# Every chunk of the SSM's GLU product as high and low halves

## What is computed

```
y = gelu(y.reshape(bsz, s, 512)).astype(u.dtype)      # 256 x 512
z_out, z_gate = split(y @ w_glu, 2, axis=-1)          # w_glu: 512 x 2048
y_ssm = z_out * sigmoid(z_gate)
```

## Time and profile before

| | |
|---|---|
| median of three runs | 1860.93 us |
| the profiled execution | 1868.62 us |
| its span | 1866.8 us |
| TensorE busy | 1796.2 us (96%) |
| VectorE busy | 1217.6 us (65%) |
| ScalarE busy | 871.8 us (47%) |
| GpSimd busy | 282.4 us (15%) |

### The profile page before, as it was taken

The page is one execution under the profiler, slowest core; times in us unless marked ns, Lnnn a source line. Parts: engine busy times, 40 slices in busy tenths (PEclk is TensorE's granted clock), DMA queues, the critical chain, the costliest instruction groups (busy, mean ns, idle before and its releaser), DMA issues.

```text
span 1866.8 us, 27009 instructions
## 1 busy us (share of the span) xinstructions
PE 1796.2 (96%) x10038; PEld 1444.8 (77%) x10038; DVE 1217.6 (65%) x1782; ACT 871.8 (47%) x1421; POOL 282.4 (15%) x278
## 2 busy tenths in 40 slices
PE   7999999989999999999989999999999999999998
PEld 6676667679998856667579998657899874779987
DVE  7997756555667893857556566545677744466775
ACT  4224445364444422436455445345655543565553
POOL 4115453010000003545111000110000001010000
PEclk9999999999999999999999999997999999799999
DMA  6445443445555444444245666431455544135553
GB/s 160 135 134 158 135 147 102 147 130 173 174 185 180 124 127 147 136 148 157 90 147 159 183 187 194 145 109 61 135 174 179 192 149 132 53 119 171 181 190 135
DMA packets 192358, 274.60 MB, mean 147 GB/s; under 512 B 25616, under 2 KB 129540, under 8 KB 192228
## 3 DMA queue, kind: packets, MB, share of 16 engines
q1 hardware_dynamic: 191364, 269.86, 46.8%
q0 software_dynamic: 864, 3.02, 0.5%
HBM read 271.78 MB, written 1.05 MB: 146 GB/s over the span
## 4 chain that ended last, share of the span: by engine, by line
PE 85%; DVE 8%; ACT 4%; issue 2%; POOL 1%; DMA 1%; DVEq 0%; ACTq 0%; SPq 0%; POOLq 0%
PE bank L402 51%; PE bank L400 23%; PE bank L590 2%; PE bank L676 2%; DVE WL L1181 2%; PE bank L1053 1%; PE bank L598 1%; PE bank L1033 1%; PE bank L492 1%; PE bank L876 1%; ACT WH L1476 1%; DVE HTL L2194 1%; DVE HTL L2111 1%; ACT HTH L1476 0%; PE bank L725 0%
## 5 line engine op out<-in xcount | busy, mean ns | idle before, releaser
L1181 DVE TENSOR_TENSOR WL<-W,WH 128x1024 fp32r<-128x1024 f32 x312 | 382.3, 1225 | 247.3 <-ACT WH L1476 238.9
L1476 ACT ACTIVATE WH<-W 128x1024 fp32r<-128x1024 f32 x332 | 351.8, 1060 | 272.8 <-PE bank L402 240.2
L402 PE MATMUL bank<-HTH,WH 128*128 128x256 f32 x1536 | 438.4, 285 | 11.6 <-issue 4.0
L402 PE MATMUL bank<-HTL,WH 128*128 128x256 f32 x1536 | 434.7, 283 | 0.0
L402 PE MATMUL bank<-HTH,WL 128*128 128x256 f32 x1536 | 434.7, 283 | 0.0
L402 PEld LDWEIGHTS bank<-HTH,WH 128*128 128x128 f32 x1536 | 294.6, 192 | 16.4 <-issue 10.0
L402 PEld LDWEIGHTS bank<-HTL,WH 128*128 128x128 f32 x1536 | 294.7, 192 | 0.2
L402 PEld LDWEIGHTS bank<-HTH,WL 128*128 128x128 f32 x1536 | 294.6, 192 | 0.0
L402 PE MATMUL bank<-WH,HTL 128*128 128x512 f32 x672 | 261.9, 407 | 0.0
L402 PE MATMUL bank<-WH,HTH 128*128 128x512 f32 x480 | 193.6, 403 | 6.9 <-DVE HTL L2194 5.0
L402 PE MATMUL bank<-WL,HTH 128*128 128x512 f32 x480 | 189.0, 394 | 0.0
(11 more groups left out here) (406 smaller groups left out, 2481.1 us busy)
## 6 DMA issues: line engine op xcount, KB each, us to landing
W<-in_w_in SPq DMA_DIRECT2D x132, 512.0 KB, 3.7
W<-in_ffn_w_gate_up SPq DMA_DIRECT2D x176, 256.0 KB, 3.4
W<-in_w_up SPq DMA_DIRECT2D x176, 256.0 KB, 3.4
W<-in_ffn_w_down SPq DMA_DIRECT2D x44, 512.0 KB, 4.2
W<-in_w_down SPq DMA_DIRECT2D x44, 512.0 KB, 4.2
W<-in_w_out SPq DMA_DIRECT2D x32, 512.0 KB, 3.3
W<-in_ssm_w_glu SPq DMA_DIRECT2D x16, 512.0 KB, 4.3
W<-in_x_w_kv SPq DMA_DIRECT2D x16, 512.0 KB, 3.8
```

Of the source, the lines that this page charges most:

```text
L402: m = pe.matmul(out, at_a(a[x]), at_b(b[y]), start=(start and i == 0), stop=(stop and i == 2), skip_group_check=True)
L1181: eng.tensor_tensor(WL[:, m % HSLOTS, 0:width], W[:, n % RSLOTS, 0:width], h, ALU.subtract)\
L1476: copy = lambda dst, src, scale=1.0: act.activation(dst, src, ACT.Copy, scale=scale)
```

## The change

All eight chunks of the GLU product go in halves. g0, g2, g4 and g6, whole before, become `"dve"` chunks: ScalarE makes their high half and VectorE the low one. GpSimd makes the halves of column tiles 0 and 1 of `UT` as well, under a new semaphore `glu_first`, for which TensorE waits ahead of `glu(0)`. In GpSimd's program this stands behind the splits of gate 3, with a wait for `y_ready` ahead of it, and the splits of gates 4 and 5 follow it.

```diff
+        glu_first = (OTR[:, 4:6, :], OTR[:, 6:8, :])
@@ token_steps (as before, with first=None)
                     if halves and k0 // kstep % 2:
                         n, w = chunk(tag, rows(wname, l, k0, kstep, c0, cols), kstep, cols, "both")
                         src, slot = halves, half_slot
+                    elif first and k0 == 0:
+                        n, w = chunk(tag, rows(wname, l, k0, kstep, c0, cols), kstep, cols, "dve")
+                        src = first
                     else:
                         n, w = chunk(tag, rows(wname, l, k0, kstep, c0, cols), kstep, cols, low)
@@ glu(h): both calls of token_out get first=glu_first
                 pe.wait_ge(sem["y_ready"], 4 * (l + 1))
+                pe.wait_ge(sem["glu_first"], l + 1)
                 pe.wait_ge(sem["glu_halves"], l + 1)
@@ gpsimd
                 signal(halves_of(mix_half, HTF, 2, 6), "mix_halves", l + 1)
+                split_to(split_before["gate", l, 3, 1])
+                pool.wait_ge(sem["y_ready"], 4 * (l + 1))
+                signal(halves_of(glu_first, UT, 0), "glu_first", l + 1)
                 split_to(split_before["gate", l, 5, 1])
                 pool.wait_ge(sem["y_ready"], 4 * (l + 1))
                 signal(halves_of(glu_half, UT, 2), "glu_halves", l + 1)
```

More of the change, by code:

```diff
@@ L408, in token_out, with token_steps @@
                     pass
-            def token_steps(tag, wname, l, act, K, c0, cols, low="dve", kstep=2, halves=None):
+            def token_steps(tag, wname, l, act, K, c0, cols, low="dve", kstep=2, halves=None, first=None):
                 ps = [begin(*tag, tt) for tt in range(TT)]
@@ L819, in glu @@
                 def glu(h):
-                    token_out(("glu", l, h, 1), "ssm_w_glu", l, UT, 4, DM + h * 512, 512, low=None, halves=glu_half)
-                    token_out(("glu", l, h, 0), "ssm_w_glu", l, UT, 4, h * 512, 512, low=None, halves=glu_half)
+                    token_out(("glu", l, h, 1), "ssm_w_glu", l, UT, 4, DM + h * 512, 512, low=None, halves=glu_half,
+                              first=glu_first)
+                    token_out(("glu", l, h, 0), "ssm_w_glu", l, UT, 4, h * 512, 512, low=None, halves=glu_half,
+                              first=glu_first)
                 def mla_in(which, tok):
```

## The result

The changed kernel takes **1908.27 us** (median of 4 runs, 1908.05 to 1915.16), against 1860.49 for the kernel before beside it (1859.37 to 1862.34): a ratio of 1.0258, 95% interval 1.0232 to 1.0284. The profiled execution took 1908.05 us. The forecast was 1906; its mechanism was right, several of its terms were not, and their errors partly met.

What follows compares the result with a forecast made beforehand. TensorE, busy for 96% of the span, was taken as the bound. The terms -5.7 + 28.7 + 4.5 + 3.5 + 14.4 gave +45.4 us on the 1860.93 us median, so 1906 us, range 1891 to 1917.

Steps and rivals of the forecast that it cites:

- part 1: GLU product on TensorE: eight chunks go from 3.44 to 2.73 us each, 5.7 us less.
- part 2: GpSimd's y_ready wait ahead of gate 4's splits: TensorE stands still 14.5 and 14.2 to 14.5 us, 28.7 in sum.
- part 3: TensorE behind the gate 4 wait: half clock loses 2.25 us in each layer, 4.5 in sum.
- part 4: Halves of g0 on ScalarE and VectorE: made in idle time ahead of g0's use, costing nothing.
- part 5: VectorE's low half of g2 in glu_out(0): late by 0.8 to 2.0 us, taken as 1.7; twice, 3.5 us.
- part 6: VectorE's low half of g6, behind norm_rows and rstd: TensorE waits 4.0 to 7.5 us, taken as 6.6; twice, 13.2.
- less at yh: Ahead of yh in layer 0: clock loss of 1.7 us goes and the shorter wait gives 1.1 us back.
- The rule on shared SBUF interfaces: GpSimd holds VectorE's operations with two SBUF inputs, so parts 5 and 6 near upper ends; without it 7 us less, 1899.
- (a): Rival: no g6 wait, because VectorE or GpSimd come to it in time; 1892 us, chance 0.14.
- (b): Rival: GpSimd's new wait is covered, gate 4 not late, only parts 1, 5 and 6 left; 1873 us, chance 0.04.
- (c): Rival: neither GpSimd's wait nor VectorE's calls come late, the 5.7 us gain is the whole; 1855 us, chance 0.03.
- (d): Rival: stages behind yh also late or clock down longer, 10 us and more over; 1920 us, chance 0.09.

Runs made afterwards that it cites:

- all_early: The changed kernel with gates 4 and 5 split ahead of the wait, g2's and g6's calls moved earlier, rstd ahead of g7's split: 1851.60 us, ratio 0.9931.
- after_again: Second profile of the changed kernel, as it is; it ran at 1909.1 us.
- gates_first: The changed kernel with GpSimd's splits of gates 4 and 5 ahead of one wait for y_ready: 1877.06 us, ratio 1.0099 to the kernel before.
- rstd_first: gates_first with GpSimd making rstd of the memory ahead of g7's split: 1871.26 us, ratio 1.0046 to the kernel before.
- before_third: Third profile of the kernel before, unchanged; it ran at 1861.1 us.
- before_again: Second profile of the kernel before, unchanged; it ran at 1866.22 us.

## Why the prediction was right, and where not

The wait, its clock and g2 and g6 are measured here from start to start of matmuls. A pair of chunks all in halves takes 5.54 us (g0 and g1, 248.31 to 253.85, where the last matmul at 253.62 gives way), a pair of a whole one and one in halves 6.17 (before, 233.22 to 239.39).

| term | forecast | measured | how |
|---|---|---|---|
| part 1, product | -5.7 | -5.0 | 8 x (6.17 - 5.54) |
| part 2, wait ahead of gate 4 | +28.7 | +29.0 | 2 x 14.5 |
| part 3, clock behind it | +4.5 | +2.5 | 1.1 and 1.4 |
| part 4, g0 | 0 | 0 | no wait |
| part 5, g2 | +3.5 | +4.7 | 2 x 2.33 |
| clock behind g2 | not in the sum | +1.6 | layer 0 alone |
| part 6, g6 | +13.2 | +16.3 | 8.14 and 8.11 |
| clock behind g6 | +4.0 | +5.1 | 2.9 and 2.2 |
| less at yh | -2.8 | -2.4 | -2.7 and +0.3 |
| sum | +45.4 | +51.8 | stage +51.3 |

- **Part 1** was mis-sized by 0.7. The forecast took 2 x 2.73 us from the chain for a pair in halves; from start to start it is 5.54, so the pair saves 0.63 us, not 0.71. In all_early's `glu(0)`, where no wait cuts the four chunks apart, it is 0.68.
- **Part 2** is right to the step. Chunk 0 begins at 202.75 and chunk 1 at 220.30, 17.55 us later, before it was 3.03 (203.19 to 206.22): 14.5 us, the forecast's number; in layer 1, 816.44 to 834.00, the same. Two smaller errors met in it: the forecast put `y_ready` at 214.5 for a chunk 1 due at 206.2, it was some 214.7 for one due at 205.8; and the halves of UT took 0.61 and 1.26 us where the earlier trace rows had 0.95 and 1.61.
- **Part 3** was put too high: the cost lies below its lower bound of 1.7 each. The 12 matmuls of chunk 1 took 4.20 us to the next chunk (220.30 to 224.50) where 3.14 stood before (206.22 to 209.36); in layer 1, 4.53 against 3.13. The windows of the changed kernel show why:

```profile
209.60:223.30 13.70, 3.00 (x7) 2.42 (x8) 4.60 (x6) 4.28 (x7) 8.15 (x6) 0.50 0.14 38
257.30:260.70 3.40, 3.40 (x10) 2.63 (x9) 0.00 (x0) 0.00 (x0) 0.00 (x0) 0.51 0.95 303
281.20:291.40 10.20, 5.98 (x14) 4.74 (x15) 4.01 (x3) 0.52 (x1) 2.81 (x3) 0.50 0.43 154
```

  The clock is at 0.50, 1.2 GHz, for 13.7 us, of which 10.7 pass while TensorE waits anyway; only 3.0 cost anything. The step that failed took the rows behind short waits for a lower bound: the longer wait had most of its half clock behind it when TensorE resumed. How much is left over differs from one execution to the next. In after_again the two stretches are 13.7 us long again, but 5.0 and 3.8 us of them lie behind the resume, and 2.0 and 1.5 us are lost.
- **Part 5** was right in its mechanism, and the cost lies over its upper bound. g2's low half took 2.47 us beside GpSimd, 253.57 to 256.04, and came 2.33 us late, not 0.8 to 2.0. It was held to the end of GpSimd's operation (254.95) and ended 1.1 us behind it, as the forecast's upper bound had it; GpSimd's end came some 0.25 us later behind g0's start than it was put, and TensorE resumed 0.14 us behind VectorE. The forecast then chose 1.7, below the end that it had worked out for a held operation. What it left out altogether is the middle row above: after a wait of 2.18 us in layer 0 TensorE ran at 0.51 for 3.4 us, 1.6 lost; after the same wait in layer 1 (2.17 us) it did not fall. In the four profiles with this wait in both layers (changed, after_again, gates_first, rstd_first) it fell behind three of the eight. The measured clock behind the earlier trace rows's wait of 2.14 us should have been carried over to this one too, with a chance.
- **Part 6** has the right chain, GpSimd's g7 split, `rstd`, `norm_rows`, g6, but came out 1.5 us too short each, past the bound of 7.5. From the best case of 4.0 us to the measured 8.1 the steps are: g7's split began 3.1 us behind g4's start (271.74 to 274.88) and not 2.7, took 3.8 us and not 3.5, `rstd` 1.5 and not 1.1. The largest is `norm_rows`, put at 0.9 to 1.8 us: it took 3.77 for its two operations, beside yh's first split on GpSimd (280.21 to 283.74). The forecast named that split, but its upper end, 1.8 us, is the length in the earlier trace rows, where GpSimd's cast and subtraction stood beside the second of the two operations only. Layer 1 of the kernel before has both nearly alone:

```profile
847.88 1.01 DVE L2085 TENSOR_SCALAR TB<-TB,RSTD 128x512 f32<-128x512 f32 x2
```

  So one is 0.49 us alone. In the changed kernel the first ended at 281.53, 0.3 us behind GpSimd's cast, and the second at 284.02, 0.3 us behind its subtraction. rstd_first shows how much of the wait is `rstd`'s place (2.0 of the 8.0 us), all_early that the rest is the place of g6's own call: there `norm_rows` still takes 3.67 us, and with g6 ahead of it no wait of g6 for its low half is left.
- **The clock of the earlier trace rows at 271.4**, which the forecast gave back at yh, is no property of the kernel before: layer 0 of before_third shows 156.4 us for the stage where before has 159.0, layer 1 of before_again has 159.0. Against before_third the change costs 53.9 us in the stage.
- **From the execution to the median.** The forecast took the 7.7 us by which the profiled execution of before lay above the median for something that stays. It was mostly the clock in the second block: both of its layers were long in that execution, 2 x 6 us, and in the changed kernel none was. before_third, which ran at the median, has one long block less, 6.0 us, and 1.6 us less ahead of it. So the execution of the changed kernel lies at its own median, the two executions differ by 39.4 us where the stages differ by 51.3, and the medians by 47.8. For the executions this is measured; that the medians differ by less than the stage for the same reason is argued from these profiles. This error (about -3.5 us in the medians) covered over half of the +5.9 by which the stage was under-estimated, and the forecast came out 2 us off. That it is so close is luck; the +45.4 against +51.3 in the stage is what the working was worth.
- **The rule on shared SBUF interfaces** was put to use for the low halves that read two tensors, and held for them: 2.47 us in place of 1.23 for g2. By the Trainium skill, GPSIMD Engine Reference, section Specifications, it is for instructions with two SBUF inputs, or in the modes with two ports. `norm_rows`, a TENSOR_SCALAR, has one tensor of 128x512 for its input, and was held as well: 3.77 us for two, 1.01 nearly alone. Whether it ran in such a mode no run here shows.
- **The rivals.** (a), g6 in time, fell with its 7.97 us. (b) and (c) fell with the wait ahead of gate 4. (d), 10 us and more over, didn't come: from the stage of layer 0 to that of layer 1 it is 429.5 us against 428.3 (one stretch of 3.4 us at half clock more, at 414.4), from there to the second block 318.2 in both. The range was given as 1891 to 1917 where the ends worked out for it are 1893 and 1918; nothing hangs on it here.

## What to carry to other kernels

Before a wait goes into an engine's program, list what is queued behind it and when the bounding engine needs each: here a wait for work that ends 10 us after the next use cost 29 us and its clock, and the whole change, which saves 5 us of product, was decided by the order of four calls. A low half, a split or any small preparation belongs ahead of the wait or norm it stands behind, as soon as its buffer is free; moving three such calls and one wait took 56 us out of the stage. Look again behind each move: `rstd` ahead of g7's split helped g6 and then, as the trace reads, made g7 late. And compare stages between landmarks, not executions: the totals of two profiles carried 12 us of something else.

## What was not expected of the hardware

- Stretches of 23.9 us at half clock in the window attention of the second block, in 5 of 22 blocks, 6 us each, with the same matmuls in the same order (229.2 against 223 us). How much of the spread of the kernel before (1853 to 1872 us in one set of runs) they make is open: of the 7.5 us between its first and third profile 6.0 are one such block, but before_again and before_third have one each and lie 5.1 us apart, by two stretches of 3.4 us at half clock in the first block.
- A wait of 2.18 us was followed by 3.4 us at 0.51 of the clock, a wait of 2.17 us at the same place a layer later by none. Behind a wait of 14.0 us the clock stayed at half for 13.7 us each time, and what that cost behind the resume was 1.1, 1.4, 1.5 and 2.0 us in two profiles.
- GpSimd's split beside VectorE held a TENSOR_SCALAR on one tensor, as it holds operations that read two: 3.77 and 3.63 us for two operations that take 1.01 nearly alone, each ending 0.3 us behind the operation of GpSimd that held it.
